# A hybrid decoder layer: the next group's front in named steps behind second halves of levels, reads copied before the inner additions, y in PSUM bank 0 behind the fourth level

## The reference

```python
def step(state, inp):
    r_t, w_t, k_t, v_t, kk_t, a_t = inp
    sa = jnp.einsum('bhvk,bhk->bhv', state, -kk_t)
    state = (state * w_t[:, :, None, :]
             + sa[..., None] * (kk_t * a_t)[:, :, None, :]
             + v_t[..., None] * k_t[:, :, None, :])
    return state, jnp.einsum('bhvk,bhk->bhv', state, r_t)
...
_, o = lax.scan(step, init, tuple(seq_first(t) for t in (r_h, w_h, k_h, v_h, kk, a_h)))
...
bonus = jnp.sum(r_h * k_h * r_k.astype(jnp.float32), axis=-1, keepdims=True) * v_h
```

## Time and profile before

| | |
|---|---|
| median of 3 runs | 2076.65 us (2076.41 to 2077.65) |
| profiled execution | 2077.94 us, span 2076.1 us |
| PE busy | 2025.1 us, 98% of the span |
| DVE busy | 1153.7 us, 56% |
| ACT busy | 860.5 us, 41% |
| POOL busy | 150.1 us, 7% |
| granted TensorE clock, mean | 0.995 |

### The profile page before, as it was taken

The page is one execution under the profiler, slowest core; times in us unless marked ns, Lnnn a source line. Parts: engine busy times, 40 slices in busy tenths (PEclk is TensorE's granted clock), DMA queues, the critical chain, the costliest instruction groups (busy, mean ns, idle before and its releaser), DMA issues.

```text
span 2076.1 us, 27660 instructions
## 1 busy us (share of the span) xinstructions
PE 2025.1 (98%) x11448; PEld 1690.4 (81%) x11448; DVE 1153.7 (56%) x1027; ACT 860.5 (41%) x833; POOL 150.1 (7%) x117
## 2 busy tenths in 40 slices
PE   8999999999999999999787999999999999999999
PEld 6888888888888888888666888888888888888887
DVE  4455555555555555757678454545555555555564
ACT  6333333333333346853333336333343333433353
POOL 0000000000000000355323200000000000000000
PEclk9999999999999999999999999999999999999999
DMA  7555555555555547656311455555555555656554
GB/s 258 186 199 185 195 186 187 197 186 196 184 188 196 182 149 223 215 182 193 106 33 49 154 186 192 183 191 193 189 195 182 192 191 184 200 182 201 183 183 142
DMA packets 190049, 373.62 MB, mean 180 GB/s; under 512 B 7110, under 2 KB 16962, under 8 KB 189980
## 3 DMA queue, kind: packets, MB, share of 16 engines
q1 hardware_dynamic: 186300, 361.47, 53.2%
q0 software_dynamic: 3680, 11.15, 1.8%
HBM read 363.94 MB, written 5.52 MB: 178 GB/s over the span
## 4 chain that ended last, share of the span: by engine, by line
PE 93%; DVE 5%; issue 2%; DMA 0%; SPq 0%; ACT 0%; DVEq 0%
PE PS L358 29%; PE PS L359 29%; PE PS L360 29%; PE PS L415 1%; PE PS L379 1%; DVE X L1626 1%; DVE XT L1639 0%; DVE wlo L344 0%; DMA x_resid<-in_x 0%; PE PS L1290 0%; PE PS L1326 0%; DVE kk L1558 0%; DVE AB L1612 0%; DVE AK L1612 0%; DVE alpha L1596 0%
## 5 line engine op out<-in xcount | busy, mean ns | idle before, releaser
L344 DVE TENSOR_TENSOR wlo<-raw,whi 128x2048 fp32r<-128x2048 f32 (+1 forms) x338 | 775.1, 2293 | 762.3 <-PE PS L360 758.3
L335 ACT ACTIVATE whi<-raw 128x2048 fp32r<-128x2048 f32 (+1 forms) x338 | 642.9, 1903 | 989.8 <-PE PS L360 985.1
L358 PE MATMUL PS<-whi,xT_hi 128*128 128x512 f32 (+2 forms) x1936 | 753.3, 389 | 0.0
L360 PE MATMUL PS<-whi,xT_lo 128*128 128x512 f32 (+2 forms) x1936 | 748.7, 387 | 0.0
L359 PE MATMUL PS<-wlo,xT_hi 128*128 128x512 f32 (+2 forms) x1936 | 748.2, 386 | 0.0
L360 PEld LDWEIGHTS PS<-whi,xT_lo 128*128 128x128 f32 x1936 | 363.6, 188 | 73.4
L358 PEld LDWEIGHTS PS<-whi,xT_hi 128*128 128x128 f32 x1936 | 363.8, 188 | 72.0 <-issue 0.4
L359 PEld LDWEIGHTS PS<-wlo,xT_hi 128*128 128x128 f32 x1936 | 363.9, 188 | 71.4
L358 PE MATMUL PS<-whi,hT_hi 128*128 128x512 f32 x680 | 265.0, 390 | 0.1
L360 PE MATMUL PS<-whi,hT_lo 128*128 128x512 f32 x680 | 264.8, 389 | 0.0
L359 PE MATMUL PS<-wlo,hT_hi 128*128 128x512 f32 x680 | 264.8, 389 | 0.0
(11 more groups left out here) (329 smaller groups left out, 1106.4 us busy)
## 6 DMA issues: line engine op xcount, KB each, us to landing
raw<-in_w_gate SPq DMA_DIRECT2D x88, 1024.0 KB, 5.1
raw<-in_w_up SPq DMA_DIRECT2D x88, 1024.0 KB, 5.1
raw<-in_w_down SPq DMA_DIRECT2D x88, 1024.0 KB, 5.1
raw<-in_w_in SPq DMA_DIRECT2D x28, 1024.0 KB, 5.8
raw<-in_w_out SPq DMA_DIRECT2D x16, 1024.0 KB, 5.1
raw<-in_w_ple_gate SPq DMA_DIRECT2D x16, 1024.0 KB, 5.0
raw<-in_w_q_b SPq DMA_DIRECT2D x3, 1024.0 KB, 5.2
z_scratch<-zst POOLq DMA_DIRECT2D x6, 512.0 KB, 3.2
```

Of the source, the lines that this page charges most:

```text
L335: nc.scalar.activation(whi[:, n % WHI, 0:wd], raw[:, n % RAW, 0:wd], ACT.Copy).then_inc(hi_ready, 1)
L344: nc.vector.tensor_tensor(wlo[:, n % WLO, 0:wd], raw[:, n % RAW, 0:wd], f32(whi[:, n % WHI, 0:wd]), ALU.subtract).then_inc(lo_ready, 1)
L358: nc.tensor.matmul(acc, a, whi[:, n % WHI, c], start=st, stop=False)
L360: ins = nc.tensor.matmul(acc, b, whi[:, n % WHI, c], start=False, stop=en)
```

## The change

The steps of `front` get names, and step 4 and 5 are each parted in two, so that there are eight steps. The later levels run front steps only behind a second half: "key" behind the third level, "own key" and "read" behind the fourth, "unit key" and "learned" behind the fifth. "read gain" and "read sum" stand in `state` behind the copy of W1T, "bonus" behind the first inner addition. `scores` is parted: the copies of the turned reads (`reads_out`) and keys (`keys_out`) come before the first and the second inner addition. y is made and copied behind the fourth level (`pe_y`, `act_y`), into one PSUM bank, bank 0, and copied to Y at once and not in two halves.

```diff
@@ pe_inverse
                         ins = by_chunks(HALF_BANKS[h][1], s, (s % 4) * CHUNK, a, half(0), b[:, s, :])
                     ins.then_inc(inv_x, 1)
+                if n == len(INV) - 2:
+                    pe_y(pe, r)
@@ 
-        def pe_state(pe, r, nxt):
+        def pe_y(pe, r):
             pe.wait_ge(ak_ready, 2 * r + 2)
             pe.wait_ge(v_handed, r + 1)
             for s, t, pr, par in systems():
                 sy, cc = head(t, pr, par)
-                ins = by_chunks(6 + t, sy, cc.start, AK, half(0), vv[:, t, cc])
+                ins = by_chunks(0, sy, t * 256 + cc.start, AK, half(0), vv[:, t, cc])
             ins.then_inc(y_done, 1)
+
+        def act_y(act, r):
+            act.wait_ge(y_done, r + 1)
+            nc.scalar.activation(Y[:, :, :].rearrange("p s c -> p (s c)"), PS[:, 0, :], ACT.Copy).then_inc(y_ready, 1)
@@ pe_state, behind W1
-            pe.wait_ge(y_ready, 2 * r + 2)
+            pe.wait_ge(y_ready, r + 1)
@@ act_inverse
                 for part in ahead(r, n):
                     act_gates(act, r + 1, part)
+                if n == len(INV) - 2:
+                    act_y(act, r)
                 if r == GROUPS - 1 and n in LATER[:2]:
@@ act_state
-            act.wait_ge(y_done, r + 1)
-            for t in range(TT):
-                nc.scalar.activation(Y[:, 4 * t:4 * t + 4, :].rearrange("p s c -> p (s c)"), PS[:, 6 + t, 0:256], ACT.Copy).then_inc(y_ready, 1)
@@ inverse (DVE)
-                        if nxt is not None:
-                            front(nxt, 2 * (n - LATER[0]) + h)
+                        if nxt is not None and h == 1:
+                            for step in {2: ("key",), 3: ("own key", "read"), 4: ("unit key", "learned")}[n]:
+                                front(nxt, step)
@@ state (DVE), behind the copy of W1T
+                if nxt is not None:
+                    front(nxt, "read gain")
+                    front(nxt, "read sum")
@@ 
-            def add_inner(r):
-                dve.wait_ge(rs_copied, 2 * r + 2)
-                for t in range(TT):
-                    dve.wait_ge(ou_done, 2 * r + t + 1)
-                    ins = v.tensor_tensor(oo[:, t, :], oo[:, t, :], PS[:, 6 + t, 0:256], ALU.add)
-                ins.then_inc(ou_read, 1)
-                dve.wait_ge(ou_read, r + 1)
+            def add_inner(r, t):
+                dve.wait_ge(rs_copied, 2 * r + t + 1)
+                dve.wait_ge(ou_done, 2 * r + t + 1)
+                v.tensor_tensor(oo[:, t, :], oo[:, t, :], PS[:, 6 + t, 0:256], ALU.add).then_inc(ou_read, 1)
@@ the loop (DVE)
                 state(it, nxt)
-                add_inner(it)
+                if nxt is not None:
+                    reads_out(nxt)
+                add_inner(it, 0)
+                if nxt is not None:
+                    front(nxt, "bonus")
+                    keys_out(nxt)
+                add_inner(it, 1)
                 if nxt is not None:
                     scores(nxt)
```

More of the change, by code:

```diff
@@ L892, in dve_w_in @@
                     dve.wait_ge(attended, 2)
-                    front(0, 0)
+                    front(0, "key")
                 if b == 20:
-                    front(0, 2)
-                    front(0, 4)
+                    front(0, "own key")
+                    front(0, "read")
+                    front(0, "read gain")
                 if b == 21:
-                    front(0, 3)
-                    front(0, 5)
+                    front(0, "unit key")
+                    front(0, "learned")
+                    front(0, "read sum")
+                    front(0, "bonus")
                 if b == 22:
@@ L1362, in pe_state @@
                 sy, cc = head(t, pr, par)
-                ins = by_chunks(6 + t, sy, cc.start, AK, half(0), vv[:, t, cc])
+                ins = by_chunks(0, sy, t * 256 + cc.start, AK, half(0), vv[:, t, cc])
             ins.then_inc(y_done, 1)
+        def act_y(act, r):
+            act.wait_ge(y_done, r + 1)
+            nc.scalar.activation(Y[:, :, :].rearrange("p s c -> p (s c)"), PS[:, 0, :], ACT.Copy).then_inc(y_ready, 1)
+        def pe_state(pe, r, nxt):
             pe.wait_ge(up_ready, 11 * r + 11)
@@ L1564, in front @@
                 r_, k_, v_ = zz[:, :, 0, :], zz[:, :, 1, :], zz[:, :, 2, :]
-                if step == 0:
+                if step == "key":
                     dve.wait_ge(*loaded(r))
@@ L1569, in front @@
                     v.reduce_sum(hsf[:, 0, :], by_head(tmn[:, :, :]), axis=X_AXIS).then_inc(kk_var, 1)
-                elif step == 3:
+                elif step == "own key":
+                    dve.wait_ge(kk_var, r + 1)
+                    dve.wait_ge(gates_ready, 2 * r + 2)
+                    chain(v.scalar_tensor_tensor(tmn[:, :, :], aa[:, :, :], -1.0, bc_t(gc[:, 1, :]), ALU.add, ALU.mult))
+                    chain(v.scalar_tensor_tensor(k2[:, :, :], tmn[:, :, :], 2.0, k_, ALU.add, ALU.mult))
+                elif step == "unit key":
                     dve.wait_ge(kk_pow, r + 1)
@@ L1574, in front @@
                     tt(by_head(kk[:, :, :]), by_head(kk[:, :, :]), per_head(hsf[:, 0, :]), ALU.mult)
+                elif step == "learned":
                     chain(v.scalar_tensor_tensor(bb[:, :, :], aa[:, :, :], 1.0, kk[:, :, :], ALU.add, ALU.mult))
[L1576 to L1581, removed]
+                elif step == "read":
                     chain(v.scalar_tensor_tensor(tmn[:, :, :], r_, 0.5, k2[:, :, :], ALU.mult, ALU.mult))
+                elif step == "read gain":
                     tt(tmn[:, :, :], tmn[:, :, :], bc_t(gc[:, 2, :]), ALU.mult)
-                elif step == 5:
+                elif step == "read sum":
                     chain(v.reduce_sum(hsf[:, 1, :], by_head(tmn[:, :, :]), axis=X_AXIS))
+                elif step == "bonus":
                     if r >= 2:
@@ L1600, in joins, with reads_out, keys_out, scores @@
                     [P, n, 32 // l, l]).bitcast(U32)
-            def scores(r):
+            def reads_out(r):
                 dve.wait_ge(turned, 4 * r + 2)
                 v.tensor_copy(ART[:, :, :, 1, :], PS[:, 0, :].rearrange("p (a t c) -> p a t c", a=2, t=TT)).then_inc(AR_v, 1)
+            def keys_out(r):
                 dve.wait_ge(turned, 4 * r + 4)
                 v.tensor_copy(KT[:, :, :], PS[:, 2, :].rearrange("p (a c) -> p a c", a=2)).then_inc(AR_v, 1)
+            def scores(r):
                 def masked(dst, mask, done, ready, b0):
@@ L1682, in state @@
                             with_decay(nxt, k)
[L1684 to L1691 removed]
+            def add_inner(r, t):
+                dve.wait_ge(rs_copied, 2 * r + t + 1)
+                dve.wait_ge(ou_done, 2 * r + t + 1)
+                v.tensor_tensor(oo[:, t, :], oo[:, t, :], PS[:, 6 + t, 0:256], ALU.add).then_inc(ou_read, 1)
             def out_centre(r):
+                dve.wait_ge(ou_read, 2 * r + 2)
                 o_ = oo[:, :, :]
@@ L1714, in dve_rwkv @@
             chain(v.memset(Q[:, :, :], 0.0))
+            reads_out(0)
+            keys_out(0)
             scores(0)
```

## The result

The changed kernel took 2065.62 us (median of 4 runs, 2065.51 to 2067.66) against 2077.15 for the kernel before on the same chips: a ratio of 0.9944, 95% interval 0.9930 to 0.9959. The forecast was 2066.4 us. The profiled span went from 2076.1 to 2065.8 us, 10.3 less, which is also what the sum said. That it agrees to a tenth is luck: the medians lie 11.5 us apart, and the second profile of the same changed kernel (e9) has a span of 2064.2 us, 11.9 less.

A forecast was written before the change was run, and what follows sets the result against it. TensorE is busy for 98% of the span, but the RWKV stage is bound by a chain of short steps across engines. 6.9 + 2 x 2.4 - 1.4 = 10.3 us gained gives 2066.4 us beside the median, range 2062.5 to 2072.0.

The forecast's parts named there:

- the sum: Whole kernel: 6.9 + 2 x 2.4 - 1.4 = 10.3 us gained; chance 0.50.
- First group, 6.9 us: First group: W1T 6.4 us earlier, less 0.35 before S, plus 0.83 at the end: 6.9 us gained.
- Middle groups, 2.4 each: Second and third group: S 1.6 us earlier and the end of the group 0.83 earlier, 2.4 gained each.
- o_ready sets level five: Middle groups: ACT's gg copy waits for og, Y and Q queue behind it; Q near 1060.85 us sets level five.
- y gains nothing: Behind level five, y's 1.2 us of products go, but that is no gain, as DVE sets W1T.
- Last group, a loss of 1.4: Last group: Y's copy on ACT delays the weight split, then DVE's split and both joins: 1.4 us lost.
- The lock of the shared port: DVE and POOL products take turns, 0.6 and 1.15 us each in middle groups; POOL undisturbed, 0.9 more gained in each.
- The front piled up before W1T: Rival: 5.4 us from last join to S instead of 3.7; kernel 4.0 slower, 2080.7 us; chance 0.05.
- The clock rival: Rival: in middle groups TensorE's slow stretch after idling covers W1 and W2, up to 1.0 us each; 2068.4 us; chance 0.13.

The follow-up runs named there:

- e4: Changed kernel with ACT's gg copy moved behind the two Q copies of level five, from the second group on: median 2068.03 us.
- e10: Changed kernel with POOL's bonus products moved behind the first turn of the next group's X into XT: median 2064.10 us.
- e11: Changed kernel with the edits of e4, e10 and e6 together: median 2059.93 us.
- e1: Changed kernel with y alone put back behind the fifth level, copied to Y in two copies: median 2066.34 us.
- e6: Changed kernel where, in the last group, ACT splits the fourth level's weight block before it copies Y: median 2066.31 us.
- e5: Changed kernel with POOL's three bonus products late, behind v_handed of the next group, in the last group behind U: median 2068.31 us.
- e8: e4 plus 80 TensorE products that nobody reads in each middle group, between W2 and the wait for W1T: median 2067.16 us.
- e3: Changed kernel with the same front steps of each later level put between its halves again: median 2079.07 us, ratio 1.0007 to the kernel before.

## Why the prediction was right, point by point

- **First group, 6.9 us: right** (43.83 - 36.91 = 6.92; 6.4 in e9's profile). By step: level four's join 1011.7 forecast, 1011.65 found (taking off 0.33 by which this execution ran late); last join of level five 1017.8 against 1017.6; W1T 1019.8 against 1020.1. Turns with POOL were as priced: k and read 1.64 us each.
- **Middle groups, 2.4 each: right** (2.52 and 2.61), with two errors that cancel. Put on the times of the kernel before, level four's join was 1054.42 (1054.5 forecast), og's end 1059.14 (1059.4), Q 1060.66 (1060.85). Level five's products took 1.60 us and not 1.92, so its joins ended at 1062.5 and not 1063.2. But the first instruction of the unit key was held by POOL for 1.14 us (0.13 when free), so W1T came at 1066.0 and not 1065.8. S was 1.5 earlier (1.6 forecast), the end of the group 1.03 (0.83). Here luck helped: the mis-sized products and the mis-sized unit key are 0.7 and 1.0 us.
- **o_ready sets level five: right as a mechanism**, shown by 6.22 us of idle ACT, 3.85 of TensorE, and e4. What the prediction did not see is how little that wait was worth: without it the gain is given back at once by the lock and by the clock (e4). Once the bonus products are out of the way it is worth 2.4 us: the third segment is 38.11 in e10 and 35.69 in e11.
- **y gains nothing: right**, by e1.
- **Last group, a loss of 1.4: right in its mechanism (e6), mis-sized.** 30.14 - 28.71 = 1.43 agrees by luck. The split's wait is 1.23. Between the last join and S, 0.50 is won back (3.51 us before, 3.01 now). Of that only 0.09 is y's, since e1, with y back there, has 3.10; before the change TensorE stood idle for 0.56 us ahead of the state step, and why is open. The remaining 0.71 lies ahead of the fourth level's join, where the clock fell in both profiles; in e9, with a clock of 1.00 there, the loss is 0.47.
- **The lock of the shared port** explains e5 and e10 as well as the sum: k and read took 1.64 us each beside POOL's products in the first group and 0.69 without them. The Trainium skill, "SBUF — State Buffer", section "Who interferes with whom", also lists tensor_scalar among the DVE operations that can run in a 2-port mode and so contend with GpSimd, with one input. The trace agrees: the one of 128x8 took 1.14 us beside POOL's product and 0.16 in e5, without it. Had I priced that step by it, W1T would have been 1.0 later in the forecast.
- **The rivals.** The front piled up before W1T did become what sets S, but level five, joined 3.3 us earlier, stood against it. The clock rival was half true: the clock did fall in both middle groups (0.66 and 0.50), but only level five's own products paid for it (1.60 us, where e4's third group took 1.15); from the last join to S DVE is busy throughout and covers the rest. What it costs in a state step, e4 against e8 shows: 0.4 and 1.3 us in the middle groups.

## What to carry to other kernels

Work that one engine does between two halves of a pipelined step also holds everything that is queued behind the second half's input: by e3 the same work, put there, made the first group 8.4 us longer up to S. Behind both halves it isn't free either, for it stands before the next step that the same engine must do; here W1T came 3.8 us behind the last join where it was 2.3. Before taking a wait away, ask what the freed engine meets next: here it was POOL's products on the shared port, and those had to be moved first. In a chain of short steps a few products that nobody reads can be cheaper than an idle TensorE (e8's state steps, 9.05 us for 9.49 and 10.36).

## What the hardware showed that I had not expected

- A DVE join of 128x256 with two SBUF inputs took 1.84 us beside a POOL product and 0.73 alone; a DVE instruction of 8 columns took 1.14 and 0.16. POOL's instruction still had 1.25 and 1.11 us to run, and the extra time was 1.1 and 1.0 us, for a long instruction and a short one alike.
- The place of TensorE's lower clock moves between executions of one program: the changed kernel's two profiles have 0.66 and 0.50 around level five of the second and third group in one and 0.50 and 0.67 in the other, and 0.72 and 1.00 in the last group's first levels. Where a state step ran in part at the lower level it was 1.2 to 1.3 us longer (10.23 us in e1, e8 and e11, 10.36 in e4, for 9.05). How much of the spread between runs of one program comes from it, no run settles.
